# A hybrid decoder layer on one core: seven products for the compressed keys' slab, and GpSimd takes steps over from VectorE

## What is computed

```python
h = rmsnorm(x, attn_norm_g[l])
(q, k_c, v_c, k_s, v_s, k_w, v_w, g_nsa, mq, mk, mv, mo, mi, mf, cu) = jnp.split(h @ w_in, points, axis=-1)
# compressed keys and values: windows of 32 tokens, 16 apart (15 windows), plus a position, through a small MLP
blk = x[:, idx] + pos[None, None, :, None, :]
kc = jax.nn.silu(blk @ w1) @ w2            # for k_c, and the same for v_c
# mLSTM: a convolution with 4 taps over (mq, mk); Conformer: one with 31 taps over ca * sigmoid(cg)
x = x + concat([attention(...), mlstm(...), conv(...)]) @ w_out
x = x + hier_moe(rmsnorm(x, ffn_norm_g[l]), ...)   # 32 experts, top 2 of one group of 8
```

## Time and profile before

| | us |
|---|---|
| median of 3 runs | 1425.35 (1424.58 to 1426.23) |
| profiled execution | 1423.53 |
| its span, first to last instruction | 1421.8 |
| PE busy | 1207.4 (85%) |
| DVE busy | 490.0 (34%) |
| ACT busy | 255.7 (18%) |
| POOL busy | 13.6 (1%) |

### The profile page before, as it was taken

One profiled execution on the slowest core, in us unless ns is written; L12 is line 12 of the kernel. 1 busy time (PEld: TensorE's weight loads), 2 busy tenths in 40 slices (PEclk: granted clock), 3 DMA queues, 4 the chain that ended last, 5 costly groups with the idle time before them and its releaser, 6 DMA issues.

```text
span 1421.8 us, 18015 instructions
## 1 busy us (share of the span) xinstructions
PE 1207.4 (85%) x7479; PEld 710.2 (50%) x7479; DVE 490.0 (34%) x1013; ACT 255.7 (18%) x629; POOL 13.6 (1%) x82
## 2 busy tenths in 40 slices
PE   8999999999999998668689958768687695876977
PEld 7999999776568753233244314224242241422422
DVE  5599997663875431121110220111101111011113
ACT  3001111444600132011111102002020020200212
POOL 2000000000010000000000000000000000000000
PEclk9999999999999999799999989989899898998989
DMA  9958567431644899999999999999999999999996
GB/s 301 324 175 173 152 151 238 118 84 35 177 108 162 350 414 428 428 428 428 427 426 429 427 428 427 428 428 427 427 428 427 427 428 427 427 428 428 429 427 262
DMA packets 133363, 479.35 MB, mean 337 GB/s; under 512 B 47804, under 2 KB 105632, under 8 KB 107552
## 3 DMA queue, kind: packets, MB, share of 16 engines
q1 hardware_dynamic: 126816, 477.58, 86.1%
q10 hardware_dynamic: 6464, 0.58, 0.4%
HBM read 476.05 MB, written 2.10 MB: 336 GB/s over the span
## 4 chain that ended last, share of the span: by engine, by line
PE 54%; DMA 42%; DVE 1%; ACT 1%; issue 1%; DVEq 0%; ACTq 0%
DMA ring<-in_expert_w_up_dram 36%; PE PS L1127 14%; PE PS L1447 10%; DMA spare<-in_expert_w_up_dram 6%; PE PS L1269 5%; PE PS L1434 4%; PE PS L1169 3%; PE PS L1246 2%; PE PS L1638 2%; PE PS L1425 1%; PE PS L1221 1%; PE PS L1648 1%; PE PS L1119 1%; PE PS L947 1%; PE PS L1188 1%; PE PS L1509 1%
## 5 line engine op out<-in xcount | busy, mean ns | idle before, releaser
L1447 PE MATMUL PS<-ring,XG 128*32 128x512 f32 x1296 | 220.7, 731 | 141.7 <-DMA ring<-in_expert_w_up_dram 102.5
L1447 PEld LDWEIGHTS PS<-ring,XG 128*32 128x32 f32 x1296 | 56.8, 130 | 267.9 <-issue 264.8
L3073 DVE TENSOR_TENSOR hTe<-PS,sg 128x128 f32<-128x128 f32 (+1 forms) x31 | 9.9, 320 | 336.5 <-ACT sg L2197 336.3
L2890 DVE TENSOR_TENSOR x<-PS,x 128x1024 f32<-128x1024 f32 x41 | 50.2, 1225 | 219.3 <-PE PS L1526 217.9
L1434 PE MATMUL PS<-ring,XG 128*64 128x512 f32 x192 | 88.0, 613 | 20.1 <-DMA ring<-in_expert_w_up_dram 17.0
L2185 ACT ACTIVATE Hs<-PS 128x512 f32<-128x512 f32 x30 | 17.9, 597 | 461.8 <-PE PS L1447 340.7
L1526 PE MATMUL PS<-Y,SW 128*128 128x512 f32 (+2 forms) x176 | 90.6, 627 | 1.7 <-ACT ro L2293 1.7
L1436 PE MATMUL PS<-ring,XG 128*64 128x512 f32 x192 | 89.7, 622 | 0.0
L1447 PE MATMUL PS<-spare,XG 128*32 128x512 f32 x208 | 64.7, 780 | 24.4 <-DMA ring<-in_expert_w_up_dram 24.4
L1425 PEld LDWEIGHTS PS<-sel,xn 128*128 128x128 f32 x640 | 75.3, 191 | 13.0 <-issue 12.7
L1127 PE MATMUL PS<-hT,ring 128*128 128x128 f32 x672 | 78.8, 275 | 0.0
(11 more groups left out here) (494 smaller groups left out, 1570.0 us busy)
## 6 DMA issues: line engine op xcount, KB each, us to landing
ring<-in_expert_w_up_dram SPq DMA_DIRECT2D x53, 2048.0 KB, 23.7
ring<-in_expert_w_gate_dram SPq DMA_DIRECT2D x53, 2048.0 KB, 26.7
ring<-in_expert_w_down_dram SPq DMA_DIRECT2D x51, 2048.0 KB, 26.6
ring<-in_w_in_dram SPq DMA_DIRECT2D x17, 2048.0 KB, 11.9
spare<-in_expert_w_gate_dram SPq DMA_DIRECT2D x9, 2048.0 KB, 26.6
spare<-in_expert_w_up_dram SPq DMA_DIRECT2D x8, 2048.0 KB, 24.0
spare<-in_expert_w_down_dram SPq DMA_DIRECT2D x8, 2048.0 KB, 27.4
ring<-in_w_in_dram SPq DMA_DIRECT2D x16, 512.0 KB, 7.2
```

The lines of the kernel that those rows point to most:

```text
L1447: mm = pe.matmul(PS[r:r + 32, 0, :], gathered_rows(q, 4 * c + j)[:, column:column + 32], weight_rows(slots[u], 4 * (c % 2) + j), start=(c ...
L2890: dve.tensor_tensor(y, new, old, ALU.add).then_inc(sc_added, 1)
```

## The change

- The slab kc0 becomes a fast slab (index 7). Its folded unit moves ahead of it and becomes unit 17; kc0's units are 18 and 19. All later fast slabs count one up: vc0 is 8, ks0 9, and so on. PSUM banks are dealt out anew between the folded and the hidden unit.
- The four weight sums of kc0 are made by POOL instead of DVE (`POOL_SUMS` is 7), from the moment PE has ended mk1.
- POOL fills `blk`: after the 4-tap convolution is done (blk lies where its input lay), it copies the eight pieces of kc0 once ACT has saved them, adds the position, and does the same for vc0. DVE waits for `blk_ready` ahead of the mLSTM's gate matrix (`gmb`), whose room holds kcv.
- The folded unit no longer waits for all units before it, only for its own inputs.
- DVE: sums 7 are gone from behind `key_taps`, `follow(7)` stands there with vc0's sums and kc0's recombination, and the convolution's steps 13 to 21 are dealt out anew (2, 2 and 4 steps in place of 5, 2 and, behind the gate matrix, 1).

```diff
-            units += [(n, part, "columns", s, 0), (n, "small", "folded", 0, 0), (n, part, "columns", s, 1)]
+            units += [(n, "small", "folded", 0, 0)] + [(n, part, "columns", s, i) for i in range(2)]
-FAST_SLABS = ("cg1", "ca0", "ca1", "mq0", "mq1", "mk0", "mk1", "vc0", "ks0", "kw0", "vs0", "q0", "q1", "q2", "q3", "vw0")
+FAST_SLABS = ("cg1", "ca0", "ca1", "mq0", "mq1", "mk0", "mk1", "kc0", "vc0", "ks0", "kw0", "vs0", "q0", "q1", "q2",
+              "q3", "vw0")
+POOL_SUMS = FAST.index(min(u for u, unit in enumerate(UNITS) if unit[1] == "kc"))
...
+    if u == FOLDED_UNIT:
+        return 6
+    if u > FOLDED_UNIT and u < HIDDEN_UNIT:
+        return (u + 3) % 4
...
+            u = FAST[POOL_SUMS]
+            n = UNITS[u][0]
+            pool.wait_ge(w_loaded[n % RING], slab_at[n])
+            pool.wait_ge(unit_done, FAST[POOL_SUMS - 1] + 2)
+            pool.tensor_tensor(in_t3, quarter(u, 1, 1), quarter(u, 0, 1), ALU.subtract).then_inc(w_summed, 1)
+            pool.wait_ge(w_summed, 4 * POOL_SUMS + 1)
+            pool.tensor_tensor(quarter(u, 0, 1), quarter(u, 0, 1), quarter(u, 0, 0), ALU.subtract).then_inc(w_summed, 1)
...
+            pool.tensor_tensor(quarter(u, 1, 0), quarter(u, 1, 0), in_t2, ALU.subtract).then_inc(w_summed, 1)
+
+            pool.wait_ge(mconv_step, 8 * ML_TAPS)
+            pool.wait_ge(par_saved, 2)
+            for b, name in enumerate(("kc", "vc")):
+                pool.wait_ge(unit_saved, units_with(name))
+                for g in range(GROUPS):
+                    for half in range(2):
...
+                        step(pool.tensor_copy(blk[64 * half:64 * half + 64, b, :, g * CMP_N:(g + 1) * CMP_N], src))
...
+                ins = pool.tensor_tensor(blk[:, b, :, :], blk[:, b, :, :], pos, ALU.add)
...
                 if kind == "folded":
                     pe.wait_ge(consts_ready, 2)
-                    pe.wait_ge(unit_saved, u - 1)
+                    pe.wait_ge(unit_saved, units_before("small") + 1)
+                    pe.wait_ge(par_saved, 2)
...
             key_taps(3, ML_TAPS)
-            left_sums(7)
-            right_sum(7)
-            last_sum(7)
-            conv_taps(13, 18)
-            follow(7)
+            follow(POOL_SUMS)
+            conv_taps(13, 15)
+            follow(8)
...
-            conv_taps(18, 20)
-            follow(8)
-
-            dve.wait_ge(mconv_step, 8 * ML_TAPS)
-            dve.wait_ge(unit_saved, units_with("vc"))
-            for b in range(2):
...
-                        step(dve.tensor_copy(blk[64 * half:64 * half + 64, b, :, g * CMP_N:(g + 1) * CMP_N], src))
...
+            conv_taps(15, 17)
             follow(9)
 
+            conv_taps(17, 21)
+            follow(10)
+
             dve.wait_ge(g_spread, 1)
+            dve.wait_ge(blk_ready, 1)
...
-            conv_taps(20, 21)
-            follow(10)
+            follow(11)
             conv_taps(21, 25)
-            follow(11)
+            follow(12)
```

More of the change, by code:

```diff
@@ L189 @@
 UNITS = projection_units()
-FAST_SLABS = ("cg1", "ca0", "ca1", "mq0", "mq1", "mk0", "mk1", "vc0", "ks0", "kw0", "vs0", "q0", "q1", "q2", "q3", "vw0")
-FAST = [u for u, (n, _, kind, _, i) in enumerate(UNITS) if SLABS[n] in FAST_SLABS and i == 0]
+FAST_SLABS = ("cg1", "ca0", "ca1", "mq0", "mq1", "mk0", "mk1", "kc0", "vc0", "ks0", "kw0", "vs0", "q0", "q1", "q2",
+              "q3", "vw0")
+FAST = [u for u, (n, _, kind, _, i) in enumerate(UNITS) if SLABS[n] in FAST_SLABS and i == 0 and kind != "folded"]
 SUMS_BEFORE, PRODUCTS_BEFORE, TOKEN_SUMS = 4 * len(FAST), 2 * len(FAST), 4
+POOL_SUMS = FAST.index(min(u for u, unit in enumerate(UNITS) if unit[1] == "kc"))
 def place_in(kind, name):
@@ L876, in _ @@
             pool.memset(m_in[:, :, 0:ML_TAPS - 1], 0.0).then_inc(consts_ready, 1)
+            u = FAST[POOL_SUMS]
[5 more added lines that the diff above has]
+            pool.tensor_tensor(quarter(u, 0, 1), quarter(u, 0, 1), quarter(u, 0, 0), ALU.subtract).then_inc(w_summed, 1)
+            pool.wait_ge(w_summed, 4 * POOL_SUMS + 2)
+            pool.tensor_tensor(in_t2, quarter(u, 1, 1), quarter(u, 0, 1), ALU.subtract).then_inc(w_summed, 1)
+            pool.wait_ge(prod_done, 2 * POOL_SUMS + 1)
+            pool.wait_ge(w_summed, 4 * POOL_SUMS + 3)
+            pool.tensor_tensor(quarter(u, 1, 0), quarter(u, 1, 0), in_t2, ALU.subtract).then_inc(w_summed, 1)
[5 more added lines that the diff above has]
+                    for half in range(2):
+                        r = 64 * (g % 2)
+                        base = kcv[r:r + 64, 2 * b + g // 2, :]
+                        src = bass.AP(base.tensor, base.offset + half, [list(base.ap[0]), [2, CMP_J], [16, CMP_N]])
+                        step(pool.tensor_copy(blk[64 * half:64 * half + 64, b, :, g * CMP_N:(g + 1) * CMP_N], src))
+                pos = par[:, PAR["pos_" + name[0]]:PAR["pos_" + name[0]] + CMP_J].unsqueeze(2).broadcast_to([P, CMP_J, 60])
+                ins = pool.tensor_tensor(blk[:, b, :, :], blk[:, b, :, :], pos, ALU.add)
+                if b == 0:
+                    step(ins)
+                else:
+                    ins.then_inc(blk_ready, 1)
             pool.wait_ge(out_done, TT)
@@ L2583, in _ @@
             dve.reciprocal(ml[:, 7, :, :], ml[:, 6, :, :]).then_inc(den_ready, 1)
[L2584 to L2587, removed]
+            keep_m1(13)
+            left_sums(14)
+            combine(13)
+            right_sum(14)
             conv_taps(25, 28)
-            last_sum(13)
+            last_sum(14)
             conv_taps(28, TAPS)
-            follow(13)
+            follow(14)
             dve.wait_ge(conv_step, TAPS * CT)
@@ L2596, in _ @@
             dve.tensor_tensor(tmp, cacc, cacc, ALU.mult).then_inc(ln_step, 1)
-            follow(14)
+            follow(15)
             dve.wait_ge(ln_step, 4)
```

3 lines of the change are left out of this document (2 added, 1 removed).

## The result

| | before | after |
|---|---|---|
| median of 6 runs, us | 1425.11 (1423.46 to 1426.23) | 1432.24 (1430.45 to 1433.13) |
| profiled execution, us | 1423.53 | 1433.13 |
| its span, us | 1421.8 | 1431.4 |
| PE busy, us | 1207.4 | 1221.2 |
| DVE busy, us | 490.0 | 498.4 |

The ratio is 1.0049 (95% interval 1.0039 to 1.0059): the changed kernel is slower by 7.1 us. The profiled executions lie 9.6 apart, as that of before is 1.6 under its median and that of after 0.9 over.

The account below looks back on a forecast made before the run. PE was taken to bound the front, DMA the experts. Terms 0.2 + 4.2 + 1.4 + 2.0 = 7.8 us made 1431.3 on the profiled 1423.53, 1433.2 on the median; range 1424.8 to 1438.5.

Parts of the forecast that it names:

- holding: DVE's SBUF steps and POOL's reads block each other for whole instructions; PE stands at vc0's m5, 4.2 us; chance 0.48.
- Entry: Ahead of kc0, PE waits 1.7 us for unit 15 to be saved; kc0 ends 0.2 us later, no gain.
- POOL's price: For kc0's weight sums on POOL, 1.8 us a sum of 1024 columns at two passes.
- break-even of 3.1: For kc0's four sums on POOL: the price a sum, in us, up to which all four are in time.
- The fill of blk: POOL's copies and additions, 4.7 us a half, beyond slack cost PE 1.4 us at ks0 and 2.0 at kw0.
- What follows: A shift at the end of the output projection carries one to one through the experts to the run's end.
- no holding: DVE's two-input steps and POOL's reads pass each other; only the entry wait counts, + 0.2 us, 1425.5; chance 0.33.
- sharing: DVE and POOL take turns column by column, each stretched by some half: + 1.5 us, 1426.9; chance 0.13.
- the delivered gain: At kc0's entry unit 15 is saved before PE asks: 1.5 us faster, 1423.8; chance 0.03.
- POOL late: At 5.0 us a sum on POOL kc0 alone is some 7 us late, 1433 or more; chance 0.03.

Follow-up runs that it names:

- entry_loose: The changed kernel, but kc0's first product asks for one saved unit fewer, so PE doesn't wait there for mk1's copy out of PSUM: 1431.30 us, ratio 1.0047.
- warm_fill: The changed kernel with five unread products of 128x512 on PE ahead of the wait for vc0's first two sums: 1431.63 us, ratio 1.0047.
- extra_sums: The kernel before, with four unread sums of 128x1024 (two SBUF inputs) on POOL from mk1's end: 1433.81 us, ratio 1.0062.
- dve_sums: The changed kernel, but DVE makes kc0's four weight sums and POOL only fills blk: 1429.59 us, ratio 1.0029.
- extra_memsets: The kernel before, with nine memsets of 128x1024 (writes, no reads) on POOL from mk1's end: 1430.38 us, ratio 1.0039.
- redealt: The changed kernel with kc0's sums on DVE, its entry asking one saved unit fewer, and DVE's convolution steps dealt out later: 1422.95 us, ratio 0.9984.
- fill_on_dve: As redealt, but DVE fills blk ahead of kw0's follow-up and three 31-tap convolution steps stand later: 1429.08 us, ratio 1.0026.
- extra_copies: The kernel before, with nine unread copies of 128x1024 (one SBUF input) on POOL from mk1's end: 1431.18 us, ratio 1.0040.

## Why the prediction came out as it did

1432.24 was measured, 1433.2 predicted, with holding as the mechanism. By its steps:

- **Entry.** PE idle was forecast from about 118.6 for 1.7 us, ended by ACT; it is 1.70, ended by ACT, and kc0 with the folded unit takes 0.6 longer than before (forecast 0.2). entry_loose adds that m5's wait takes over whatever is saved here.
- **POOL's price.** Assumed 1.8 us a sum, measured 2.35 to 2.41, a third more, but below the break-even of 3.1, so that kc0 itself finds its sums in time, as forecast. The estimate of 2.2 worked out from the figure of the Trainium skill, GPSIMD Engine Reference, section Performance versus the Vector engine (4497 ns for 2048 columns), was nearer than the step of the sum.
- **Holding.** The forecast was 4 x 1.8 less 1.4 of `combine(6)`, 5.8 us of delay on DVE. The delay is 8.84 - 1.66 = 7.2. Two terms were mis-sized, one against the other: the sums are dearer (9.8 us from 119.01 to 128.84), and DVE's own four steps, 1.66, fit into the turns between them, which the sum did not take off: less the 1.3 of `combine(6)` that lie beside them (to 120.28), 9.8 - 1.3 - 1.66 is 6.8. That `combine(6)`, which reads PSUM, runs on was right. PE's wait at m5 was forecast at 4.2 and is 5.2.
- **The fill of blk.** Forecast: 4.7 us of delay a half, 1.4 at ks0 and 2.0 at kw0. The delays are 3.9 and 3.2 (7.17 and 6.50 less 3.25), and PE waits at neither. The copies are dearer than the 0.38 assumed (6.68 / 8 = 0.84, turns included), but only what falls on DVE's steps of the moment counts. At full clock (warm_fill) the two waits are 0.32 and 0.80.
- **The clock, a term that was missing.** 1.9 us for the four products behind the standing. Nothing in the sum stood for it.
- **What follows.** One to one to the experts: 8.2 at vc0's end, 8.36 at the first expert load. As forecast.

In all 0.6 + 5.2 + 1.9 + 0 makes 7.7 where the forecast had 0.2 + 4.2 + 1.4 + 2.0, 7.8. The mechanism and the place of its largest term are shown (extra_sums, dve_sums); that the total is so near owes much to terms that cancel: 3.4 us of fill that did not come, against 1.0 of standing, 1.9 of clock and 0.4 of entry that were not in it. That is luck. Of the rivals, no holding and sharing fall by the same row (8.84 us); the delivered gain falls at the entry; POOL late falls by 2.4 us a sum. The rows that stood against holding were of pairs in which POOL read no SBUF or DVE read PSUM; extra_memsets shows for the first that with two-input steps this makes the difference, and `combine(6)` beside POOL's first sum for the second. The chances that the prediction counts as slower (0.48, 0.03 and 0.09) add up to 0.60, where it writes 0.58.

## What to carry to other kernels

Work given from VectorE to GpSimd is free for VectorE only while VectorE runs something that doesn't share: four sums of 1.25 us each took 7.2 us from it when they ran on GpSimd beside its SBUF steps, and 5.0 when it made them itself. Before moving a step, write down when each input is wanted and how much slack the giving engine has at that point; with the list dealt out by these times and the entry wait loosened the same change went from 7 us slower to 2 us faster, and then it no longer mattered which engine made the sums. Where TensorE is the bound, count for a wait of some microseconds also the slower products that may come behind it.

## What the runs showed of the hardware that was not expected

- **Turns, not rates.** Beside a POOL instruction that shares with it, a DVE step of 0.41 us costs a whole POOL instruction: 8.84 / 4 = 2.21 us beside sums of 2.35 to 2.41. Of a long DVE instruction the turns take a smaller share: beside POOL's copies the short steps took 0.90 (7.17 / 8) in place of 0.41, a sum of 1024 columns in redealt 1.51 in place of 1.23. DVE in redealt:

```profile
145.39 1.51 DVE L2416 TENSOR_TENSOR ring<-ring 128x1024 f32<-128x1024 f32 x1
```

- **Memsets hold one-input steps.** 8 `tensor_scalar` of 128x256 took 6.94 us in place of 2.67 beside memsets of 9.36 / 9 = 1.04 us.
- **The clock after a wait.** The windows of extra_memsets at the end of PE's standing:

```profile
139.00:141.00 2.00, 0.37 (x1) 0.38 (x2) 1.93 (x3) 0.00 (x0) 0.00 (x0) 0.76 1.35 217
141.00:143.00 2.00, 2.00 (x11) 2.00 (x11) 1.90 (x2) 0.00 (x0) 0.00 (x0) 0.50 1.32 213
```

  It fell to the 1.2 GHz level in a standing of 2.6 us there, and in those of 4.05 (fill_on_dve), 4.4 (extra_copies), 5.2 (after), 5.5 (extra_sums) and 7.1 (entry_loose). It stayed at 2.4 GHz through 2.99 us in dve_sums and where products filled most of the gap (warm_fill). 2.6 and 2.99 stand the wrong way round, so the length of the standing alone does not decide; what does is left open.
